# Both feed-forwards of a two-layer hybrid model as seven block products in place of eight, with 288-column matmuls

## What is computed

```python
def sq_relu_ffn(x, g, w1, w2):            # w1: 1024 x 4096, w2: 4096 x 1024
    h = jax.nn.relu(rmsnorm(x, g) @ w1)
    return (h * h) @ w2
...
        xp = xp + yp
        xs = xs + ys
        xp = xp + sq_relu_ffn(xp, norm_ffn_g[l], w_ff1[l], w_ff2[l])
```

## Time and profile before

| | us |
|---|---|
| three runs, median (lowest to highest) | 2799.99 (2798.99 to 2803.66) |
| span of the profiled execution | 2805.1 |
| PE busy | 2748.7 (98%) |
| weight loads busy | 2669.0 (95%) |
| DVE busy | 1044.2 (37%) |
| POOL busy | 858.5 (31%) |
| ACT busy | 532.9 (19%) |

### The profile page before, as it was taken

One profiled execution on the slowest core, in us unless ns is written; L12 is line 12 of the kernel. 1 busy time (PEld: TensorE's weight loads), 2 busy tenths in 40 slices (PEclk: granted clock), 3 DMA queues, 4 the chain that ended last, 5 costly groups with the idle time before them and its releaser, 6 DMA issues.

```text
span 2805.1 us, 38166 instructions
## 1 busy us (share of the span) xinstructions
PE 2748.7 (98%) x15795; PEld 2669.0 (95%) x15795; DVE 1044.2 (37%) x1410; ACT 532.9 (19%) x916; POOL 858.5 (31%) x732
## 2 busy tenths in 40 slices
PE   7999999999999999999999999989999999999998
PEld 7997699999999999999999898979999999999998
DVE  5217935221221222157646464653522222212215
ACT  3113622010010001022323223231301100100103
POOL 6543422232222222223222222252222222322222
PEclk9999989999999999999999999999999999999999
DMA  6321021111111111122232232432111111111112
GB/s 193 72 54 31 4 105 38 38 45 45 45 37 45 40 42 45 38 104 72 36 104 42 86 63 72 81 115 105 46 38 45 41 41 37 45 45 45 37 45 75
DMA packets 109410, 164.01 MB, mean 58 GB/s; under 512 B 55820, under 2 KB 70156, under 8 KB 108544
## 3 DMA queue, kind: packets, MB, share of 16 engines
q1 hardware_dynamic: 35536, 105.05, 12.7%
q10 hardware_dynamic: 73504, 56.60, 7.2%
q0 software_dynamic: 272, 0.98, 0.1%
HBM read 132.81 MB, written 24.49 MB: 56 GB/s over the span
## 4 chain that ended last, share of the span: by engine, by line
PE 94%; DVE 3%; DMA 1%; issue 1%; ACT 1%; POOL 0%; ACTq 0%; DVEq 0%; POOLq 0%
PE psum L629 78%; PE psum L961 4%; PE psum L728 2%; PE psum L656 1%; PE psum L1003 1%; PE psum L1037 1%; PE psum L1043 1%; PE psum L993 1%; PE psum L809 1%; DMA out_qk_s<-high 1%; PE psum L850 1%; DVE low L1495 1%; PE psum L985 1%; DVE low L1499 0%; PE psum L973 0%
## 5 line engine op out<-in xcount | busy, mean ns | idle before, releaser
L452 POOL TENSOR_SCALAR w_hi<-w_raw 128x1024 fp32r<-128x1024 f32 x191 | 205.0, 1073 | 1594.5 <-PE psum L629 1319.8
L629 PE MATMUL psum<-a_hi,w_hi 128*128 128x384 f32 x2808 | 651.8, 339 | 18.7 <-DVE a_lo L1137 17.3
L629 PE MATMUL psum<-a_lo,w_hi 128*128 128x384 f32 x2808 | 640.0, 335 | 0.0
L629 PE MATMUL psum<-a_hi,w_lo 128*128 128x384 f32 x2808 | 639.7, 335 | 0.0
L629 PEld LDWEIGHTS psum<-a_hi,w_hi 128*128 128x128 f32 x2808 | 499.0, 189 | 26.7 <-issue 14.5
L629 PEld LDWEIGHTS psum<-a_hi,w_lo 128*128 128x128 f32 x2808 | 502.8, 188 | 0.0
L629 PEld LDWEIGHTS psum<-a_lo,w_hi 128*128 128x128 f32 x2808 | 502.0, 188 | 0.0
L455 POOL TENSOR_TENSOR w_lo<-w_raw,w_hi 128x1024 fp32r<-128x1024 f32 x191 | 460.8, 2413 | 15.9
L1171 DVE TENSOR_TENSOR low<-psum,low 128x1152 f32<-128x1152 f32 x142 | 192.8, 1358 | 608.7 <-PE psum L629 608.5
L629 PE MATMUL psum<-h_hi,w_hi 128*128 128x384 f32 x1512 | 343.0, 334 | 0.0
L629 PE MATMUL psum<-h_lo,w_hi 128*128 128x384 f32 x1512 | 343.0, 334 | 0.0
(11 more groups left out here) (236 smaller groups left out, 2281.3 us busy)
## 6 DMA issues: line engine op xcount, KB each, us to landing
w_raw<-in_wall SPq DMA_DIRECT2D x191, 512.0 KB, 3.3
low<-in_x ACTq DMA_DIRECT2D x16, 576.0 KB, 8.7
high<-in_mem_in ACTq DMA_DIRECT2D x32, 257.0 KB, 4.1
out_mem_s<-high ACTq DMA_DIRECT2D x32, 257.0 KB, 3.3
out_x_spill<-low ACTq DMA_DIRECT2D x8, 576.0 KB, 2.7
low<-out_x_spill ACTq DMA_DIRECT2D x8, 576.0 KB, 7.6
out_y<-low SPq DMA_DIRECT2D x22, 192.0 KB, 2.3
out_mix_spill<-mid ACTq DMA_DIRECT2D x3, 1152.0 KB, 4.5
```

Source lines behind the costliest of these rows:

```text
L452: nc.gpsimd.tensor_scalar(w_hi[:, s, :], w_raw[:, s, :], 1.0, 1.0, ALU.mult, ALU.mult)\
L629: r = mm(psum[:, z + i, 0:TN], w[:, s, k * P:(k + 1) * P], a[:, kk, tok(i)], start=first and n == 0, stop=last and n == 2)
```

## The change

Both feed-forwards are cut two by two by two: weights, activations and result each into four blocks, and the product of the blocks is made of seven block products of sums and differences in place of eight plain ones.

*Operands.* The tokens are cut into two halves of 576 (`HN`), each half into two matmuls of 288 columns (`QT`). Up: the 1024 input channels are cut 512 / 512, and the hidden tiles are taken in pairs (16 pairs a layer, `PAIRS`). Seven right operands (B11, B21, B22, and T1 to T4, sums of the blocks of the scaled `x`) are made once a layer from `x`, split, and kept for all pairs. Down: a chunk's 512 hidden channels are two groups of two tiles, and the output tiles are taken in pairs (32 units a layer, `DUNITS`). The seven right operands are the four hidden blocks and four sums, one of the eight not needed.

*Weights.* SP loads the same units as before, two per up pair and one per down unit. POOL makes four sums of the blocks for each group of seven, of 512 columns (up) or 256 (down), in place and in `spare`; ACT now writes the high parts, POOL the low parts, each block into its own slot of a ring in `w_hi` and `w_lo`: 4 slots up, 8 down.

*Products.* An up product is 4 k-tiles x 3 passes x 2 = 24 matmuls, a down product 12. Both stages have 7 x 16 x 24 = 7 x 32 x 12 = 2688 matmuls a layer. The last down unit of layer 1 stays a plain product, made in quarters of the tokens (`last_pair`, 96 matmuls in place of 84). PE accumulates three or four products in one pair of banks and waits in between until DVE (or ACT, `copied`) has read the running sum.

*Sums of the results.* DVE joins the products (`joined`, 4 a pair), applies relu and scale (4), and makes the sums T1 to T4 of the squared hidden tiles (4); ACT copies two running sums out and squares four blocks, all 576 columns wide. The seven blocks of each pair are written to DRAM (`keep`, 288 KB each, 16 x 7 a layer) and come back a chunk at a time (`rows_in`, 576 KB each, 8 x 7 a layer); ACT writes their high parts (`rows_high`, 1152 columns) and DVE the low parts (`rows_low`, two of 576). In the down stage DVE adds the running sum to half a tile of `x` after each of the seven products. The upper half of `x` waits in DRAM meanwhile (`x_hold`).

*Entry.* The output projection makes its tiles in the order 0, 4, 1, 5, 2, 6, 3, 7, and the operands are made while it runs. `token_sums` comes after the second product of the first pair. All of the feed-forwards' code is unrolled in place of loops. The end of the kernel works in quarters of 288 tokens, its column sums in groups of 96. Elsewhere counters are shared between stages, with no other change.

```diff
+HN = T // 2
+QT = T // 4
+UP = (1, 5, 6, 2, 7, 3, 4)
+DOWN = (1, 2, 6, 5, 7, 3, 4)
+OPERAND = {1: "B11", 2: "B21", 3: "B22", 4: "T4", 5: "T1", 6: "T2", 7: "T3"}
+HELD = ("B11", "B21", "B22", "T1", "T2", "T3", "T4")
+SUMS = {7: 1, 5: 2, 6: 3, 3: 4}
+PAIRS, DUNITS = FC * FK // 2, FC * 4
+NPU, NPD = 7 * PAIRS, 7 * DUNITS
+NP = NPU + NPD
...
+OUTS = (0, 4, 1, 5, 2, 6, 3, 7)
+FIRST = [(o, k) for k in range(3) for o in ("T1", "T2", "T4")]
+LATER = [("B11", k) for k in range(4)] + [(o, k) for o in ("B21", "B22") for k in range(3)]
...
+        def up_banks(f, p):
+            return (0, 2, 4, 6) if (p + f) % 2 == 0 else (6, 2, 4, 0)
+
+        def down_banks(f, d):
+            at = 6 * f
+            return (at, 2, 4) if d % 2 == 0 else (4, 2, at)
...
+                def keep(p, o):
+                    sp.dma_start(ffn_rows[p // 2, HELD.index(o), :, p % 2, :], kept[o])\
+                        .then_inc({"B11": c_out, "B22": c_out, "T4": t4_out}.get(o, up_out), 16)
...
+            def low_weights(f, n, src):
+
+                at = slot(f, n)
+                pool.wait_ge(f_high, NP * f + n + 1)
+                nc.gpsimd.tensor_tensor(w_lo_flat[:, at], src, w_hi_flat[:, at].bitcast(F32), ALU.subtract)\
+                    .then_inc(f_split, 1)
+
+            def combine(f, n):
+
+                order = UP if n < NPU else DOWN
+                a11, a12, a21, a22 = raw_blocks(n)
+                s3 = spare[:, 0:512 if n < NPU else 256]
+                g = 4 * ((PAIRS + DUNITS) * f + n // 7)
+
+                def low_of(product, src):
+                    low_weights(f, n + order.index(product), src)
+
+                def summed(dst, one, other, op):
+                    nc.gpsimd.tensor_tensor(dst, one, other, op).then_inc(f_sum, 1)
+
+                low_of(1, a11)
+                if n >= NPU:
+                    low_of(2, a12)
+                if f or n:
+                    pool.wait_ge(f_split, NP * f + n - 2)
+                summed(s3, a11, a21, ALU.subtract)
+                pool.wait_ge(f_sum, g + 1)
+                summed(a21, a21, a22, ALU.add)
+                if n < NPU:
+                    low_of(5, a21)
+                pool.wait_ge(f_split, NP * f + n + 1)
+                pool.wait_ge(f_sum, g + 2)
+                summed(a11, a21, a11, ALU.subtract)
+                low_of(6, a11)
+                low_of(*((2, a12) if n < NPU else (5, a21)))
+                pool.wait_ge(f_split, NP * f + n + order.index(2) + 1)
+                pool.wait_ge(f_sum, g + 3)
+                summed(a12, a12, a11, ALU.subtract)
+                low_of(7, s3)
+                low_of(3, a12)
+                low_of(4, a22)
...
+            def product(bank, at, k_tiles, rows, start, stop, ready=None):
+
+                for k in range(k_tiles):
+                    if ready is not None:
+                        ready(k)
+                    for n, (v, part) in enumerate(((w_hi_flat, 0), (w_hi_flat, 1), (w_lo_flat, 0))):
+                        for i in range(2):
+                            r = mm(psum[:, bank + i, 0:QT], v[:, at.start + P * k:at.start + P * (k + 1)],
+                                   rows(part, k)[:, qtok(i)], start=start and k == 0 and n == 0,
+                                   stop=stop and k == k_tiles - 1 and n == 2, skip_group_check=True)
+                r.then_inc(f_done, 1)
...
+                    product(X, at, kt, rows, True, False, ready)
+                    at, kt, rows, ready = begin(1)
+                    if first:
+                        pe.wait_ge(evicted, b_out + 8)
+                    else:
+                        pe.wait_ge(up_read, r0 + 4 * p)
+                    product(V, at, kt, rows, True, True, ready)
+                    if first:
+                        token_sums(sums, 2 * f + 1, W)
+                    at, kt, rows, ready = begin(2)
+                    pe.wait_ge(copied, 2 * (PAIRS * f + p) + 1)
+                    product(X, at, kt, rows, False, False, ready)
+                    at, kt, rows, ready = begin(3)
+                    product(Z, at, kt, rows, True, True, ready)
+                    at, kt, rows, ready = begin(4)
+                    pe.wait_ge(up_read, r0 + 4 * p + 1)
+                    product(X, at, kt, rows, False, False, ready)
+                    at, kt, rows, ready = begin(5)
+                    product(V, at, kt, rows, True, True, ready)
+                    at, kt, rows, ready = begin(6)
+                    pe.wait_ge(up_read, r0 + 4 * p + 3)
+                    product(X, at, kt, rows, False, True, ready)
...
+                    if d == 0:
+                        pe.wait_ge(c_relu, 4 * (PAIRS * f + PAIRS - 1))
+                    else:
+                        pe.wait_ge(dn_read, d0 + 7 * (d - 1) + 6)
+                    product(X, *begin(0), True, False)
+                    if d == 0:
+                        pe.wait_ge(up_read, r0 + 4 * PAIRS)
+                    product(Z, *begin(1), True, True)
+                    pe.wait_ge(dn_read, d0 + 7 * d + 1)
+                    product(X, *begin(2), False, False)
+                    product(V, *begin(3), True, False)
+                    pe.wait_ge(dn_read, d0 + 7 * d + 3)
+                    product(X, *begin(4), False, False)
+                    pe.wait_ge(dn_read, d0 + 7 * d + 4)
+                    product(V, *begin(5), False, True)
+                    pe.wait_ge(dn_read, d0 + 7 * d + 5)
+                    product(X, *begin(6), False, True)
...
+                    dve.wait_ge(copied, 2 * (p0 + p) + 2)
+                    dve.wait_ge(f_done, done + 3)
+                    joined(c12, c22, two(X))
+                    if final:
+                        rows_low(0, 0)
+                    dve.wait_ge(f_done, done + 4)
+                    joined(c11, c11, two(Z))
+                    if first:
+                        dve.wait_ge(aux_read, sums + NT)
+                        V.reciprocal(rbc[:, tok(0)], rbc[:, tok(0)]).then_inc(ff_sum, 1)
+                    else:
+                        dve.wait_ge(up_read, at + 2)
+                        relu(c11, 0)
+                    if final:
+                        rows_low(0, 1)
+                    dve.wait_ge(f_done, done + 5)
+                    joined(c22, c22, two(X))
+                    if first:
+                        V.reciprocal(rbc[:, tok(1)], rbc[:, tok(1)]).then_inc(ff_sum, 1)
+                    else:
+                        dve.wait_ge(up_read, at + 3)
+                        relu(c22, 1)
+                    if final:
+                        rows_low(0, 2)
+                    dve.wait_ge(f_done, done + 6)
+                    joined(c12, c12, two(V_))
+                    dve.wait_ge(up_read, at + 4)
+                    if first:
+                        V.reciprocal(rbc[:, tok(2)], rbc[:, tok(2)]).then_inc(ff_sum, 1)
+                        dve.wait_ge(ff_root, f + 1)
+                        relu(c11, 0)
+                        relu(c22, 1)
+                    relu(c12, 1)
+                    dve.wait_ge(h_sq, sq + 3)
+                    t_sum(ct1, c12, c11)
+                    if final:
+                        rows_low(0, 3)
+                    else:
+                        late_sums(p, 0)
+                        late_sums(p, 1)
+                    dve.wait_ge(f_done, done + 7)
+                    relu(c21, 0, two(X))
...
+                    places = ((0, 0, X), (0, 0, Z), (0, 1, X), (1, 1, V_), (1, 1, X), (0, 1, V_), (1, 0, X))
+                    for i, (o, h, bank) in enumerate(places):
+                        k = 2 * j + o
+                        if c == 0 and k >= 4 and i in (0, 3):
+                            dve.wait_ge(x_in[k], 48 + 32 * f)
+                        dve.wait_ge(f_done, done + i + 1)
+                        if i in (1, 4):
+                            dve.wait_ge(dn_read, at + i)
+                        dst = by2(x[:, k, half(h)])
+                        V.tensor_tensor(dst, dst, two(bank), ALU.add).then_inc(dn_read, 1)
+                        q = 7 * j + i
+                        if d == 0 and i in (0, 2, 4):
+                            rows_low(0, 4 + i // 2)
+                        if d == 0 and i in (1, 3, 5):
+                            late_sums(PAIRS - 1, i // 2)
+                        if c == 0 and q >= 7 and q % 3 != 0:
+                            rows_low(1, (q - 7) // 3, ((q - 7) % 3,))
+                        elif 0 < c < FC - 1 and q % 4 >= 2:
+                            rows_low(c + 1, q // 4, (q % 4 - 2,))
...
+                    if n < RING_UP:
+                        act.wait_ge(block_done, b_out + 7 + n // 2)
+                    elif up:
+                        act.wait_ge(f_done, n0 + n - RING_UP + 1)
+                    elif n < NPU + RING_DOWN:
+                        act.wait_ge(f_done, n0 + NPU - RING_UP + (n - NPU) // 2 + 1)
+                    else:
+                        act.wait_ge(f_done, n0 + n - RING_DOWN + 1)
```

(3 more changed lines are left out.)

1018 lines of the change are left out of this document (736 added, 282 removed).

## The result

The changed kernel takes 2779.25 us (median of 4 runs, 2777.36 to 2784.48; the profiled execution was the longest of them) against 2799.66 us: a ratio of 0.9924, interval 0.991 to 0.9938. It is faster by 20 us; the forecast was 2695 us with a range of 2640 to 2750. The sign was right, the size was not.

The account below looks back on a forecast made before the run. The prediction took PE's matmul pace to bound the kernel (PE busy 98% of the span). Its terms, -162.3 + 21.4 + 6.6 + 10 + 16 + 3.5 = -104.8 us, gave a forecast of 2695 us, range 2640 to 2750.

Parts of the forecast that it names:

- matmul term: Feed-forward matmuls: 10764 at 133.33 ns in place of 9216 at 173.34, with a constant 13.3 ns surplus: -162.3 us.
- steady pairs (2 to 14): Up stage: each operation has at least one product (3.2 us) until PE needs its answer, so no loss: 0.
- steady down units (2 to 29): Down stage: row splits on DVE wait for POOL, 0.25 us a unit over 63 units: +16 us.
- entry (pair 0): Start of each feed-forward: PE waits for the token sums, then runs at lower clock: +10.7 us, twice.
- second pair: Second up pair: the first pair's reciprocals, table load and root delay ACT's copy: +3.3 us, twice.
- up to down (pair 15, units 0, 1): Change of stage: chunk 0's operands return through few staging places, so low parts come late: +5 us, twice.
- last units and tail: Last down units and kernel end: extra row splits and square additions on DVE, the tail's quarters giving -1: +3.5 us.
- a shared surplus (130.0): Rival on matmul pace: the surplus is a share of the columns, 130.0 ns a matmul: 2659 us, chance 12%.
- of 2.5 ns: Rival on matmul pace: the surplus falls to 2.5 ns a matmul: 2579 us, chance 3%.
- weight loads (143 or more): Rival: weight loads hold matmuls at 173 ns, 3126 us, chance 5%; above 143.1 ns the change loses.
- POOL and DVE bound the down stage: Rival: a down unit takes 12.0 us against PE's 11.2, 50 us in place of 16: 2729 us, chance 17%.
- Of its signs: Down-stage signs of that rival: PE waiting on POOL's `w_lo`; POOL's 256-column subtraction above 0.72 us under the lock.

Follow-up runs that it names:

- e15_store: Fastest earlier kernel doing only useful work (2719 us), with the store of B22's block ahead of the next weight loads in the first pair: 2708.21 us.
- e2_relu: Changed kernel with VectorE's relu of C21 ahead of the first two late sums, in every pair but the last: 2747.6 us.
- e4_narrow: Changed kernel with work left out: GpSimd's low parts of the feed-forward weights for 64 columns of each slot alone: 2723.42 us, one run.
- e5_reload_relu: Changed kernel with e2_relu's order, weight loads of down units 2 and 3 issued earlier, and the x_hold reloads behind both: 2728.41 us.
- e12_narrow: e5_reload_relu with work left out: GpSimd's low parts of the weights for 64 columns of each slot alone: 2702.08 us, one run.
- e1_reload: Changed kernel with the four x_hold reloads moved behind the weight loads of down units 2 and 3: 2768.04 us.
- e11_warm2: e5_reload_relu with useless TensorE matmuls filling its waits, as in e8_warm but without the six ahead of the first pair's third product: 2721.65 us.
- e7_lows: Changed kernel with work left out: VectorE's low parts of the entry's B operands and some first down rows for 32 columns alone: 2763.85 us, one run.
- e8_warm: Changed kernel with useless TensorE matmuls added where it stood idle, in the first two pairs and the first down unit: 2779.59 us.
- e9_recip: e5_reload_relu with VectorE's three reciprocals in the first pair one product earlier: 2726.7 us.

## Why the prediction was wrong

By its own steps, for both feed-forwards together (excess over the matmuls in the profiled execution, from the edges of the stages):

| step | forecast us | measured us |
|---|---|---|
| matmul term | -162.3 | 133.3 ns a matmul, as forecast |
| steady pairs (2 to 14) | 0 | +31.1 |
| steady down units (2 to 29) | +16 | +1.5 |
| entry (pair 0) | +22 | +32 |
| second pair | +6.6 | +15.5 |
| up to down (pair 15, units 0, 1) | +10 | +54 |
| last units and tail | +3.5 | +10 |

Behind the matmul term the measured ones make 144 to 145 us in place of 58; the difference, 86 us, is the miss (82.4 us in span) but for 4.8 us that the stretch between the feed-forwards gave back and 0.7 that the one ahead of them took.

**Right: the matmul term.** The surplus of 13.3 ns, taken as a constant by the form of plain f32, gave the right pace at 288 columns. The rivals of a shared surplus (130.0), of 2.5 ns and of weight loads (143 or more) are ruled out as this kernel's pace by the 11.20 us of a unit. As a law of the matmul a constant is not shown: at half clock the matmuls stood 240 ns apart, which is 288 columns at 1.2 GHz and no surplus, and 130.0 ns was seen in 14 of 440 groups of twelve in this kernel's second feed-forward and in a whole stage of e15_store. The Trainium skill ("TensorE: Matmul & The Clock Gate", Back-to-back issue gap) would give 122.5 ns, or 10.3 us a unit; no row here shows it.

**Wrong: "Steady up pairs: 0".** The step said that each operation has "at least one product (3.2 us) until PE needs the answer". That counts each operation by itself. The seventh product's answer is needed after 6.4 us (two products of the next pair), and four things stand in series there: sums ahead of the relu, the relu, the square, the copy (4.88 + 0.74 + 0.68 + 0.63 = 6.93 us in the rows above). The lock that I read in the earlier trace rows and priced at 0.25 us a split in the down stage was left out of the up stage, where the sums and the relus with both inputs in SBUF took 1375 and 1640 ns against 785 and 807. e2_relu and e4_narrow show both halves. The cover named was there; the order used it up.

**Wrong: "Up to down: +5 us".** My schedule traced the row parts only. The excess is 26.2 and 28.1 us, and some 9 of it was the weight load of the third unit behind the last stores and 2.3 MB of reloads, shown by e5_reload_relu against e2_relu (70.5 to 61.1 us, 69.4 to 61.0). The prediction asked of each queue what the moved steps wait for, but SyncE's queue was followed for rows and not for weights. For the 16 us that are left then, e12_narrow shows 4.1 (4.5 in the second feed-forward) to be GpSimd's; the rest (late row loads, for which ScalarE waited 7.02 and 4.06 us in e1_reload, with the additions behind) is argued and not shown.

**Too small: the entry and the second pair.** The mechanism of the entry was as told: the last residual stands behind ten low parts, and the token sums behind the work that follows. The hand schedule, whose zero is 12.5 us before the projection's end at 462.98, had that residual end at 17.9; it ended at 23.2. These rows of VectorE and TensorE answer it:

```profile
460.50 11.92 DVE L1559 SCALAR_TENSOR_TENSOR a_lo<-low,cols,a_hi 128x576 fp32r<-128x576 f32 x10 [5.19 <-ACT a_hi L2266]
472.35 1.34 DVE L1549 TENSOR_TENSOR low<-psum,low 128x1152 f32<-128x1152 f32 x1
...
473.79 1.30 PE L987 MATMUL psum<-op_h,w_hi 128*128 128x288 f32 x4 [7.46 <-issue]
```

Mis-sized were the ten low parts (11.92 us, not 7.6: they met GpSimd's sums, and ScalarE's high parts ahead of them) and what stands behind them: PE waited 7.46 us for the second product already, and 3.62 for the read of the sums. GpSimd's part in it is shown by e4_narrow: 36.2 us for the pair. 39.7 - 24.3 - 7.46 - 3.62 leaves 4.3 us, nearly all of it half clock (32 matmuls at 240 ns in place of 133.3 are 3.4 us more), where 1.7 were put down; e11_warm2 shows that these were no loss of their own, since the pair kept its 39.8 us without most of them. That VectorE's list set the pair's length is shown in part: e7_lows, with less work in it, has 34.6. In the second pair the sum had the reciprocals, the table load and the root, but not the half clock behind the wait (2.7 us by e8_warm). In the changed kernel the squares and the stores end there within 0.7 us of each other, which is why e9_recip, moving one of them, gained nothing, and e15_store, moving the second when the first had gone, gained 4.5 us in that pair (26.9 to 22.4).

**Wrong to the good side: the down units.** A row split delayed by GpSimd costs PE nothing, since the lead of a product takes it; the lower bound, nothing, was the better value. The rival "POOL and DVE bound the down stage" is ruled out: 11.2 us a unit from the sixth on. Of its signs one came: GpSimd's 256-column subtraction took 804 ns in the mean where 0.72 us was named, and it cost PE nothing.

**Last units and tail: +10 in place of +3.5.** The last two units of layer 0 took 4.7 us over their matmuls where 3 were put down for three, layer 1's last whole unit 1.1. From its end to the end of the kernel it is 35.1 us where 30.4 were, 1.1 of it a wait ahead of `last_pair`: 4.6 in place of -1. VectorE comes to it with squares still to add. No run changed this; it is read from the time line only.

## What to carry to other kernels

When a faster engine leaves others the same answers to give in less time, don't compare each operation with its slack: follow for each buffer the whole series from a product to the next use, through every engine's list and the DMA queue, with all that stands ahead in each. Price an operation of VectorE with both inputs in SBUF beside a busy GpSimd at up to twice its time, from the first pair on. And when the wait at the end of a chain is taken away and nothing happens, look for a second one that ended at the same time before calling it the amount of work.
